# A three-stage transformer kernel: query projections ahead of keys in the latent attention, head pairs turned during its second half, the differential heads' ends in pieces, and merged key and bonus products in the chunk loop

## The reference, cut to what matters

```
# latent attention, first block
down = h @ w_down                       # 384 query, 256 key-value, 32 rotary columns
q  = rmsnorm(down[:, :384]) @ w_uq      # 16 heads of 64 + 32
kv = rmsnorm(down[:, 384:640]) @ w_ukv  # 16 heads of 64 + 64
s  = (q_nope k_nope + rope(q_rope) rope(k_rope)) * 96**-0.5, causal
x  = x + (softmax(s) @ v) @ w_o

# second block: eight score matrices, two to each differential head of width 128
attn = softmax(s1) - lam * softmax(s2);  o = attn @ v;  o = rms_norm(o) * (1 - lam_init)
# and beside it, per head and time step
state = state * w_t + (state @ -kk_t) (kk_t * a_t) + v_t k_t;  y_t = state @ r_t
y = y + sum(r * k * r_k) * v            # the bonus
```

## Time and profile before

| what | us |
|---|---|
| runs, median (lowest to highest) | 2125.57 (2125.27 to 2130.46) |
| the profiled execution, its own time | 2130.16 |
| span of the profiled execution | 2128.4 |
| PE busy | 2024.5 (95%) |
| DVE busy | 1021.7 (48%) |
| ACT busy | 762.8 (36%) |
| POOL busy | 208.7 (10%) |
| mean granted TensorE clock | 0.973 |

### The profile page before, as it was taken

One profiled execution on the slowest core, in us unless ns is written; L12 is line 12 of the kernel. 1 busy time (PEld: TensorE's weight loads), 2 busy tenths in 40 slices (PEclk: granted clock), 3 DMA queues, 4 the chain that ended last, 5 costly groups with the idle time before them and its releaser, 6 DMA issues.

```text
span 2128.4 us, 25332 instructions
## 1 busy us (share of the span) xinstructions
PE 2024.5 (95%) x9936; PEld 1660.5 (78%) x9936; DVE 1021.7 (48%) x1365; ACT 762.8 (36%) x1142; POOL 208.7 (10%) x254
## 2 busy tenths in 40 slices
PE   8999899999999899899999999989889979999997
PEld 6876688888888677788888887868689858888886
DVE  5444444343346645344343337566543366666534
ACT  3235432222224454432222225253433334333322
POOL 4000010000002201010000003012722030000000
PEclk9999899999999999899999999999999999999998
DMA  6210023232222101033233233311120113233221
GB/s 186 91 40 6 21 82 111 84 99 99 99 91 71 54 21 40 20 92 108 81 97 98 99 99 90 99 60 42 39 40 2 40 40 112 86 99 99 99 99 39
DMA packets 140700, 158.10 MB, mean 74 GB/s; under 512 B 15944, under 2 KB 129616, under 8 KB 140624
## 3 DMA queue, kind: packets, MB, share of 16 engines
q1 hardware_dynamic: 139328, 155.01, 23.0%
q0 software_dynamic: 1296, 2.05, 0.4%
HBM read 153.36 MB, written 3.68 MB: 74 GB/s over the span
## 4 chain that ended last, share of the span: by engine, by line
PE 85%; DVE 9%; ACT 3%; issue 2%; DMA 0%; POOL 0%; SPq 0%; DVEq 0%; ACTq 0%; POOLq 0%
PE bank L2591 33%; PE bank L2611 15%; PE bank L2234 14%; PE bank L2259 3%; PE bank L2322 3%; PE bank L2352 2%; PE bank L2630 2%; DVE XL L1468 1%; PE bank L2338 1%; PE bank L2570 1%; ACT w_hi L960 1%; PE bank L2432 1%; PE bank L2395 1%; PE bank L2846 1%; DVE w_lo L1461 1%
## 5 line engine op out<-in xcount | busy, mean ns | idle before, releaser
L2591 PE MATMUL bank<-XH,w_hi 128*128 128x512 f32 x1008 | 398.9, 396 | 0.0
L2591 PE MATMUL bank<-XH,w_lo 128*128 128x512 f32 x1008 | 393.6, 390 | 0.0
L2591 PE MATMUL bank<-XL,w_hi 128*128 128x512 f32 x1008 | 393.4, 390 | 0.0
L2591 PEld LDWEIGHTS bank<-XH,w_hi 128*128 128x128 f32 x1008 | 189.4, 188 | 41.0 <-issue 0.5
L2591 PEld LDWEIGHTS bank<-XH,w_lo 128*128 128x128 f32 x1008 | 189.2, 188 | 39.8
L2591 PEld LDWEIGHTS bank<-XL,w_hi 128*128 128x128 f32 x1008 | 189.5, 188 | 38.7 <-issue 0.5
L2234 PE MATMUL bank<-XH,w_hi 128*128 128x512 f32 x512 | 206.1, 402 | 6.5 <-DVE w_lo L1461 2.1
L2234 PE MATMUL bank<-XL,w_hi 128*128 128x512 f32 x512 | 201.9, 394 | 0.0
L2234 PE MATMUL bank<-XH,w_lo 128*128 128x512 f32 x512 | 201.8, 394 | 0.0
L2611 PE MATMUL bank<-XL,w_hi 128*128 128x512 f32 x480 | 186.9, 389 | 0.0
L2611 PE MATMUL bank<-XH,w_hi 128*128 128x512 f32 x480 | 186.8, 389 | 0.0
(11 more groups left out here) (402 smaller groups left out, 3408.1 us busy)
## 6 DMA issues: line engine op xcount, KB each, us to landing
w_raw<-in_ffn_w_gate SPq DMA_DIRECT2D x22, 1024.0 KB, 5.3
w_raw<-in_ffn_w_up SPq DMA_DIRECT2D x22, 1024.0 KB, 5.4
w_raw<-in_ffn_w_down SPq DMA_DIRECT2D x22, 1024.0 KB, 4.9
w_raw<-in_w_up SPq DMA_DIRECT2D x22, 1024.0 KB, 5.0
w_raw<-in_w_in SPq DMA_DIRECT2D x13, 1024.0 KB, 5.3
w_raw<-in_w_down SPq DMA_DIRECT2D x11, 1024.0 KB, 5.0
w_raw<-in_even_w_in SPq DMA_DIRECT2D x9, 1024.0 KB, 5.4
w_raw<-in_even_w_out SPq DMA_DIRECT2D x4, 1024.0 KB, 5.0
```

The costliest lines, as they stand in the source:

```text
L2591: m = pe.matmul(bank[b][:, :], w[:, k, P * c:P * (c + 1)], x[:, k, :], start=(k == 0 and j == 0), stop=(k == KT - 1 and j == 2))
```

## The change

In `mla` the units of the down product come in the order of the columns (query first). In each half the two query units stand before the key-value unit. The query root goes to `rstd1` and the key-value root to `rstd`. `attention` may start when all but the last `vm` tile has been taken out. Seven of the eight head pairs are turned inside the second half's attention (`MLA_TURNS`, through bank 7); the eighth follows it, and the first tile of `mla_out` takes that pair last. In `attention("diff")` the odd head's subtraction, square and sum are put into three later groups. In the chunk loop `keys(c)` multiplies `KKbd` once with 128 columns (keys and receptances side by side, `KRrk`), and the bonus is one product with `half_ones` over 256 columns, POOL having multiplied by `r_k` first. `off_diagonal(0)` stands before `turn(0)`, on ACT too.

```diff
             w = d["mla_w_down"][0]
-            for n0, n in ((512, 160), (256, 256), (0, 256)):
+            for n0, n in ((0, 256), (256, 256), (512, 160)):
                 units.append(("mla_down", rows(w, 0, KT, n0, n)))
             for half in range(2):
+                linear(f"mla_q{half}", d["mla_w_uq"][0][:, 768 * half:768 * (half + 1)], 768, 384, 3)
                 units.append((f"mla_kv{half}", rows(d["mla_w_ukv"][0], 0, 2, 1024 * half, 1024)))
-                linear(f"mla_q{half}", d["mla_w_uq"][0][:, 768 * half:768 * (half + 1)], 768, 384, 3)
             linear("mla_out", d["mla_w_o"][0], D)
...
-NORMS = [("even", 8), ("ffn0", 8), ("mla", 8), ("kv", 2), ("q", 3), ("ffn1", 8), ("pre", 8), ("post", 8), ("fpre", 8),
+NORMS = [("even", 8), ("ffn0", 8), ("mla", 8), ("q", 3), ("kv", 2), ("ffn1", 8), ("pre", 8), ("post", 8), ("fpre", 8),
...
+        KRrk = arena[:, base1:base1 + 8 * SEQ].rearrange("p (a t s) -> p a t s", a=2, t=4)
...
+        MLA_TURNS = {2: 0, 5: 1, 8: 2, 11: 3, 14: 4, 17: 5, 21: 6}
...
+                        r_k = V("r_k_2", 0, 4).unsqueeze(2).broadcast_to([P, 4, CH])
+                        link(pool.tensor_tensor(bonus_in, KRr[:, :, chunk(c)], kk[:, :, chunk(c)], ALU.mult))
+                        pool.tensor_tensor(bonus_in, bonus_in, r_k, ALU.mult).then_inc(rw_bq, 1)
...
+            def head_pair_high(t):
+                act.wait_ge(ot_turned, ot_base["mla"] + t + 1)
+                act.activation(XH[:, t, :], bank[7][:, :], ACT.Copy).then_inc(ot_hi, 1)
...
+                    if half == 0:
+                        attention("mla0")
+                attention("mla1", lambda n: head_pair_high(MLA_TURNS[n - 1]) if n - 1 in MLA_TURNS else None)
+                head_pair_high(7)
                 residual("mla_out", "ffn1")
...
+                off_diagonal(0)
                 token_major(0)
-                off_diagonal(0)
...
-                    if name == "diff" and h % 2:
-                        dve.wait_ge(at_on, hh + 1)
-                        full = otok_d[:, :, 128 * (h // 2):128 * (h // 2) + 128]
-                        link(dve.tensor_tensor(full, full, odt, ALU.subtract))
-                        link(dve.tensor_tensor(odt, full, full, ALU.mult))
-                        last = dve.tensor_reduce(ssd[:, 4 * (h // 2):4 * (h // 2) + 4], odt, AX.X, ALU.add)
...
+                def difference(h):
+                    full = otok_d[:, :, 128 * (h // 2):128 * (h // 2) + 128]
+                    dve.wait_ge(at_on, h0 + h + 1)
+                    link(dve.tensor_tensor(full, full, odt, ALU.subtract))
...
+                def squared(h):
+                    full = otok_d[:, :, 128 * (h // 2):128 * (h // 2) + 128]
+                    link(dve.tensor_tensor(odt, full, full, ALU.mult))
+
+                def square_sum(h):
+                    last = dve.tensor_reduce(ssd[:, 4 * (h // 2):4 * (h // 2) + 4], odt, AX.X, ALU.add)
+                    if h == 7:
+                        last.then_inc(sub_sum, 1)
+                    else:
+                        link(last)
 
                 for n, (h, gi, tiles) in enumerate(groups):
                     maxima(n)
                     if gi == 1 and h >= 1:
                         head_end(h - 1)
+                    if name == "diff" and gi == 2 and h >= 2 and h % 2 == 0:
+                        difference(h - 1)
+                    if name == "diff" and gi == 0 and h >= 3 and h % 2:
+                        squared(h - 2)
+                    if name == "diff" and gi == 1 and h >= 3 and h % 2:
+                        square_sum(h - 2)
                     between(n)
                 head_end(7)
+                if name == "diff":
+                    difference(7)
+                    squared(7)
+                    square_sum(7)
...
+            def head_pair_low(t):
+                dve.wait_ge(ot_hi, ot_base["mla"] + t + 1)
+                dve.tensor_tensor(XL[:, t, :], bank[7][:, :], XH[:, t, :].bitcast(F32), ALU.subtract).then_inc(ot_lo, 1)
...
+                            if half == 0 and h == 0:
+                                dve.wait_ge(rstd_ready, norm_use["kv"] + 1)
+                                for n in range(2):
+                                    dve.scalar_tensor_tensor(cq[:, 3 + n, :], cq[:, 3 + n, :], V("mla_kv_norm", n), rstd,
+                                                             ALU.mult, ALU.mult).then_inc(kv_normed, 1)
+                        if half == 0 and u == first["mla_q0"]:
+                            for n in range(2):
+                                dve.wait_ge(norm_hi, split_base["kv"] + n + 1)
+                                dve.tensor_tensor(XL[:, 3 + n, :], cq[:, 3 + n, :], XH[:, 3 + n, :].bitcast(F32),
+                                                  ALU.subtract).then_inc(norm_lo, 1)
...
+                        if half == 0:
+                            columns(2)
+                            dve.tensor_scalar(qs, rcol, 96.0 ** -0.5, None, ALU.mult)
+                            link(dve.tensor_scalar(nqs, rcol, -(96.0 ** -0.5), None, ALU.mult))
+                        for t in range(4):
+                            dve.wait_ge(lin_ready, L + 1)
+                            dve.tensor_copy(vm[:, t, :], bank[L % 4][:, :]).then_inc(lin_free, 1)
+                            L += 1
...
-                    if n == 23:
-                        for t in range(4):
-                            m = dve.tensor_scalar(bonus_w[:, t, :], C("half_ones"), V("r_k_2", t), None, ALU.mult)
-                        m.then_inc(rw_bw, 1)
...
+                            rows, name = late[1], late[0]
+                            pe.wait_ge(ot_lo, ot_base[name] + min(rows.values()) - 1)
+                            for p, k in enumerate([k for k in range(KT) if k not in rows] + list(rows)):
+                                if k in rows:
+                                    pe.wait_ge(ot_lo, ot_base[name] + rows[k])
...
-                pe.wait_ge(at_on, h0 + (8 if name != "diff" else 7))
+                pe.wait_ge(at_on, h0 + (8 if name == "mla0" else 7))
...
+            def turn_pair(t):
+
+                pe.wait_ge(at_on, ATT["mla1"]["h0"] + max(2 * t - 6, 0))
+                if t >= 1:
+                    pe.wait_ge(ot_lo, ot_base["mla"] + t)
+                for i in range(ST):
+                    m = pe.transpose(bank[7][:, P * i:P * (i + 1)], otok_m[:, i, P * t:P * (t + 1)], ident)
+                m.then_inc(ot_turned, 1)
...
-                    pe.wait_ge(lin_free, L)
+                    pe.wait_ge(lin_free, L - 1)
...
-                    if half == 0:
-                        pe.wait_ge(rcol_ready, 1)
-                    attention(f"mla{half}")
+
+                    def between(n):
+                        if n == -1:
+                            pe.wait_ge(lin_free, L)
+                        if half and n in MLA_TURNS:
+                            turn_pair(MLA_TURNS[n])
+
+                    attention(f"mla{half}", between)
                     if half == 0:
...
-                turn_pairs("mla", otok_m, lambda t: (at_on, ATT["mla1"]["h0"] + 8))
-                linear("mla_out", L, release=True)
+                turn_pair(7)
+                linear("mla_out", L, release=True, late=("mla", {7: 8}))
...
                         pe.matmul(bank[4][:, part(t)], AAbd[:, t, :], KRr[:, t, chunk(c)], start=True, stop=True)
-                        pe.matmul(bank[4][:, part(4 + t)], KKbd[:, t, :], KRk[:, t, chunk(c)], start=True, stop=True)
-                        pe.matmul(bank[5][:, part(t)], KKbd[:, t, :], KRr[:, t, chunk(c)], start=True, stop=True)
-                    pe.wait_ge(rw_bw, 1)
+                        pe.matmul(bank[5][:, part(t, P)].rearrange("p (a b) -> p a b", a=2), KKbd[:, t, :],
+                                  KRrk[:, :, t, chunk(c)], start=True, stop=True)
                     pe.wait_ge(rw_bq, c + 1)
-                    for t in range(4):
-                        m = pe.matmul(bank[5][:, part(4 + t)], bonus_w[:, t, :], bonus_in[:, t, :], start=True, stop=True)
-                    m.then_inc(rw_a2, 1)
+                    pe.matmul(bank[4][:, 4 * CH:8 * CH], C("half_ones"), bonus_in, start=True, stop=True).then_inc(rw_a2, 1)
...
                 keys(0)
+                off_diagonal(0)
                 turn(0)
-                off_diagonal(0)
```

More of the change, by code:

```diff
@@ L369, in build @@
         rw_bq = sem("rw_bq")
-        rw_bw = sem("rw_bw")
         rw_al = sem("rw_al")
@@ L2280, in linear @@
                             hi, lo = wv(u, 256, KT)
-                            for p, k in enumerate([k for k in range(KT) if k not in late] + list(late)):
-                                if k in late:
-                                    pe.wait_ge(ot_lo, ot_base["even"] + late[k])
+                            rows, name = late[1], late[0]
[3 more added lines that the diff above has]
+                                    pe.wait_ge(ot_lo, ot_base[name] + rows[k])
```

(4 more changed lines are left out.)

196 lines of the change are left out of this document (76 added, 120 removed).

## The result

| | before | after |
|---|---|---|
| median of four runs each, us | 2128.02 | 2097.36 |
| lowest to highest | 2125.27 to 2130.61 | 2093.24 to 2099.87 |
| span of the profiled execution | 2128.4 | 2096.7 |
| mean granted clock | 0.973 | 0.977 |

The ratio after to before is 0.9854 (95% interval 0.9831 to 0.9878): faster by about 31 us. The forecast was 2090, in a range of 2079 to 2102. It had been taken off a median of 2125.57 for the kernel before; off the 2128.02 of this table the same 35.2 us give 2093.

A forecast was written before the change was run, and what follows sets the result against it. PE, busy for 95% of the span, was taken to bound the kernel. Terms 12.7 + 7.2 + 7.0 - 0.7 + 9.0 = 35.2 us, taken off the median 2125.57, gave 2090 us, range 2079 to 2102.

The forecast's parts named there:

- First half: Latent attention's first half: waits of 2.03, 2.74 and 4.38 us and low-clock stretches go, 12.7 us less; bounds 9 and 13.5.
- PE's first token tile 0.7 us late: First half's projections: `kc` copies stand behind query heads and weight splits on DVE, so the first token tile comes 0.7 us late.
- Second half: Latent attention's second half: the 4.68 us wait and the low-clock opening go, 7.2 us less; bounds 4 and 8.
- Head pairs: Turns around the second half's attention: 10.3 us less behind it, 3.6 us more inside, 7 us less; bounds 3.1 and 9.
- Differential attention: Differential attention and start of chunks: attention ends some 11 us earlier, but POOL and transfers swallow it; 0.7 us more.
- Rival 1: Differential attention's gain reaches the end: 11 us more go, 2079 us; chance 0.09.
- POOL was to lose 0.7 us beside DVE: End of POOL's inversion: the last odd head's DVE subtraction and square beside POOL's copy cost POOL twice 0.35 us.
- 34.5 and 35.3: Sums of savings in us if POOL loses 1.5 us by the port rule, or 0.7 us by the trace.
- a stretch at the low level: Start of the chunks: PE's long idle time may add low-clock time, the 4 us bound of the term.
- Chunk loop: Merged key product saves 0.88 us and bonus 0.41 us per chunk, seven times: 9.0 us less; bounds 5.5 and 9.5.
- Rival 2: Latent attention gives less: clock falls at both openings, each turn adds 1.3 us; 2100 us, chance 0.22.
- no new wait over 1 us in the projections: Sign in the latent attention's projections: the four old PE waits gone and no new one above 1 us.

The follow-up runs named there:

- copies_first: Changed kernel with DVE's split of the next weights behind the four `kc` copies of each half instead of ahead: 2091.51 us, ratio 0.9828.
- turns_behind: Changed kernel with all eight head pairs turned behind the second half's attention in two banks: 2098.59 us, ratio 0.9861.
- pieces_back: Changed kernel with the odd differential heads' subtraction, square and sum right behind the head's division again: 2091.99 us, ratio 0.9830.
- half_inversion: Changed kernel with 16 of the 31 steps of POOL's inversion, so the inverses are not complete: 2082.83 us, ratio 0.9788.
- fillers: Changed kernel with 24 unread 512-column products on PE, 17 before `keys(0)` and 7 before `off_diagonal(0)`: 2095.96 us, ratio 0.9849.
- keys_apart: Changed kernel with the merged 128-column key product made as two of 64 columns again: 2100.48 us, ratio 0.9868.
- inverse_first: Changed kernel with DVE memsets, `turn(0)` first, `kc` copies before split, six unread products, second inverse's transfers first on SP: 2079.55 us, ratio 0.9781.
- zeros_on_dve: Changed kernel with the three memsets behind POOL's inversion made by DVE ahead of the last head's division: 2090.36 us, ratio 0.9825.

## Why the prediction was right, and where it was off

**First half.** The mechanism held: the three waits went and the attention opened at full clock. The term was -12.7 and came out at -10.3. The step that was off is "I follow DVE's queue from there and find PE's first token tile 0.7 us late": PE waits 1.18 and 1.64 us there, 2.1 us more than the 0.7. For the 1.64 us the split was named as the cause, and copies_first shows it by moving it. The 1.18 us end with a product of DVE on a query head (L1946), and stayed in copies_first. No run puts the old order of the units back; that the order is what removed the three waits rests on the rows.

**Second half.** -7.2 forecast. The projections gave -3.7 of it directly. The attention's opening gives the rest: -9.4 for the stretch, of which the turns are -6.8 (-10.4 behind it, +3.1 for seven groups and +0.5 at the last head in it), leaves -2.6. So -6.3.

**Head pairs.** -7.0 forecast, -6.8 by that account, and turns_behind measured 6.6. Its price of 0.44 us for a group is what a head grew by (5.79 to 6.23).

**Differential attention.** The attention ends 10.7 us earlier, as forecast. The claim that this gain is swallowed by POOL is shown by pieces_back (PE's waits move, `off_diagonal(0)` hardly) and by half_inversion (shorten POOL, and the gain arrives). Rival 1 is out. Two steps inside the +0.7 were off. First, POOL was to lose 0.7 us beside DVE; the memsets came 0.07 us later. What the trace has instead is DVE losing. Its last subtraction, beside POOL's copy (1514.32 to 1516.23), took 1.66 us where others took 0.69:

```profile
1515.13 1.66 DVE L1521 TENSOR_TENSOR under_split<-under_split,arena 128x512 f32<-128x512 f32 x1
```

All four such subtractions, asked by their line (durations in ns, shortest, median, longest):

```profile
L1521 DVE TENSOR_TENSOR under_split<-under_split,arena x4: 687/687/1658, 1476.7 to 1515.1; 128x512 f32<-128x512 f32 x4
```

The rule of the Trainium skill (SBUF — State Buffer, Who interferes with whom), that one of the two blocks the other, fits this row. That POOL would be the one to lose, 1.5 us, was my own reading of it and did not happen: the same section of the Trainium skill says that the order of issue decides who waits, and POOL's copy had started 0.81 us before. (The prediction's sums in that passage, 34.5 and 35.3, should read 34.4 and 35.2 by its own terms.) Second, the clock: "a stretch at the low level" was only a bound of the term. Here PE ran at it for all of `keys(0)` and on to 1538, and fillers and pieces_back price it at 3.5 to 3.7 us between `off_diagonal(0)` and the first product. The total stayed at +0.1 for two reasons. PE takes its work up again at nearly the same distance from the opening: 78.33 before, with `turn(0)` next, and 78.11 after, with `off_diagonal(0)` next. And the same work from there to the first product took 9.83 us before and 10.19 after, since the kernel before ran at the low clock in most of it too. The forecast had the mechanism. That the new idle time's low clock added only 0.4 us here is in part luck, since equal code gave first products from 86.7 to 88.3. So in the changed kernel the pieces are worth nothing or cost up to 2.6 us. With equal code spread over 1.6 us, that size stays open.

**Chunk loop.** -9.0 forecast, -9.35 measured; a chunk, from `keys(c)` to `keys(c + 1)`, takes 12.47 us instead of 13.83. Both loops have one stretch of some 3.4 us at 0.50. keys_apart prices the key half at 6.2 us (0.88 a chunk), as the sum had it; the bonus by itself was not run.

**Rivals and signs.** Rival 2 (the latent attention gives less) had the right direction for the first half, but not its mechanism: the clock did not fall at either opening and a turn added 0.44 us, not 1.3; DVE's queue was late. Of the signs named, "no new wait over 1 us in the projections" failed twice (1.18 and 1.64 us). PE's idle time ahead of `blocks(0)` was 8.43 us and ahead of `off_diagonal(0)` 3.85, where some 6 us each were named.

**The rest.** The group norm and what follows took 0.9 us more and the start 0.3 us more, with code that the change doesn't touch; 456.0 to 457.8 us are found for the former among all kernels. In the spans the whole is -31.7 against -35.2: 2.4 us of the difference are the first half, 0.9 the second, 0.2 the pairs, 1.2 these two; the other stretches came out some 1.2 us better than forecast.

## What to carry to other kernels

Before an engine's stall is removed, follow what its end releases: here 11 us of attention time ended in a wait for another engine's serial chain, and the work behind the standstill ran at half clock, 3.7 us dearer. Shorten that chain first (take its memsets away, send first what is needed first), and then the early end pays: inverse_first, which also fills the waits with products that nobody reads, made 10 us of it. When whole times spread as much as the gain looked for, cut the profiles at fixed rows and compare the stretches.

## What was not expected of the hardware

- Four transfers issued by a second engine beside eight others landed 5.0 us after issue in the median, 8.6 at most, instead of 3.5 and 4.1. The next weights travelled beside them too, and which of these is the cause stays open. Against zeros_on_dve, which kept one queue, `off_diagonal(0)` even came 0.9 us later (76.87 against 75.99).
- DVE made the three memsets no faster than POOL: 5.9 us from the first's start to the last's end in zeros_on_dve, against 5.3 in the changed kernel.
- The granted clock rose to 1.00 while PE was idle (1514 to 1518) and was back at 0.50 before PE's next product at 1522.32.
- Code at equal places ran with or without stretches at 0.50 from one profile to the next. The chunk loop took 97.12 us, or 98.75, or 100.40, the same values in all kernels to within 0.02 us (keys_apart aside): with no such stretch near its start, a short one, or a longer one.
